# An SSM norm factor moved behind the projection, and the first weight chunk in pieces on two queues

## The chip, the cores and the metric

One core of one Trainium2 chip. The metric is the device time of one execution in microseconds; before and after are the medians of several runs.

## The reference, cut to what matters

The kernel computes a chain of float32 blocks over 256 tokens of width 1024. First comes an SSM layer with a pooling branch, then a SwiGLU feed-forward (ffn0), an attention layer, a second SwiGLU feed-forward (ffn1), a gated short convolution and a squared-ReLU MLP. The change is in the first layer:

```
proj = x @ w_in                                  # w_in: 1024 x 3088
u, z, xbc, dt = split(proj)
y_pool = multiscale_pool(u, pool_w, pool_scale)  # 256 x 512
y = ssd(xbc, dt, ...) + xh * d_skip              # 256 x 1024
y = y * silu(z)
y_ssm = y * rsqrt(mean(y*y, axis=-1) + 1e-6) * norm_w
h = concat([y_pool, y_ssm], axis=-1) @ w_out     # 1536 x 1024
x = layer_norm(ALPHA * x + h, g, b)              # ln0, then ffn0
```

The factor rsqrt(mean(y*y)) is one number per token, norm_w one number per channel.

## The kernel before

**Weights.** All weights pass through one list of chunks, mostly 1 MB each: either 1024 rows x 256 columns ("column chunk", 8 k tiles of 128 rows, in runs of 1 KB) or 256 rows x 1024 columns ("row chunk"). Chunk 0 is the dt part of w_in, 16 columns (64 KB, runs of 64 bytes); chunks 1 to 12 are the rest of w_in, 13 to 18 w_out (13, 14 the pool half, 15 to 18 the SSM half, called q = 0 to 3), 19 on ffn0. SyncE issues them in this order into four, later six slots, each when an earlier chunk's slot is free (L444 to L452). ScalarE copies each chunk rounded into `hi` (L1106), VectorE makes `lo = raw - hi` (L1519), both in program order by calls `split(n)`, "up to chunk n". TensorE makes three matmuls for each product: hi*hi, hi*lo, lo*hi (L551 to L563).

**Start.** SyncE issues x (two halves) and then chunks 0, 1, 2, 3. ScalarE issues the identity, two rows of vectors and the other constants (L1202 to L1205, 656 KB). GpSimd issues small vectors, two strided d_skip broadcasts (L482), the pooling weight (L484) and two lnrow broadcasts of 512 KB (L466). TensorE transposes x (L733), ScalarE and VectorE make x_hi and x_lo, and then come column blocks 0, 1, three small transposes and blocks 2 to 12 (`col`, L565). ScalarE evacuates each block, VectorE runs the convolution (L1740, L1742).

**End of the SSM stage.** PSUM banks 0 to 3 take the output of w_out, token-major: 128 tokens of half h in banks 2h and 2h+1. TensorE adds the pool rows first (`rows_full` of chunks 13 and 14, L851 and L857). VectorE finishes y (L1810) and multiplies by silu(z) (L1821). Then ScalarE squares (L1119), VectorE folds (L1535, L1538), TensorE sums over channels (L663), ScalarE takes the root (L1125), VectorE inverts (L1543), TensorE broadcasts the factor over partitions (L674), VectorE scales y (L1549), ScalarE makes x_hi with the gain (L1133), VectorE makes the full product and x_lo (L1567, L1558). Only then do the SSM rows run: half 0 over q = 0 to 3, then half 1, with the transposes of ln0's first half (`turn`, L647) ahead of the last twelve matmuls. ln0 itself is on VectorE (L1581 to L1601): `ALPHA * x + PSUM`, statistics, normalise. ffn0 opens with blocks of one token half at a time (`half_cols`, L581) in banks 6, 7 and 4, 5.

Of the kernel before, what the change touches and what calls it, by code (L numbers as in the profile page):

```python
# [11 lines left out]
P = 128  # L12
# [3 lines left out]
KT = D // P  # L16
# [53 lines left out]
def build(nc, A, out):  # L70
    ctx = ExitStack()
    with ctx:
# [25 lines left out]
        d_skip = sb("d_skip_sb", [P, KT])  # L98
        head_vec = sb("head_vec", [16, 4])
# [219 lines left out]
        def norm_incs(name, kind):  # L319

            pairs = NORM_TILES[name] // 2
            if kind == "folded":
# [13 lines left out]
        NORM_BANKS = {"qn": (7, 7), "kvn": (7, 7), "ssm": (5, 6)}  # L336
# [103 lines left out]
        def _(sp):  # L440
# [3 lines left out]
            for c in range(n_chunks):  # L444
# [16 lines left out]
        def _(pool):  # L461
# [14 lines left out]
            with nc.allow_non_contiguous_dma(reason="a few small vectors"):  # L476
# [72 lines left out]
        def _(pe):  # L549
# [15 lines left out]
            def col(c, bank, hi, lo, operand=None, between=None):  # L565
# [3 lines left out]
                pe.wait_ge(lo_split, c + 1)  # L569
                for m in range(0, n, P):  # L570
# [3 lines left out]
                    for k in range(kt):  # L574
                        if operand and m == 0 and k % 2 == 0:
# [36 lines left out]
            def rows_full(c, hi, lo, start):  # L612

                rows_part(c, hi, lo, 0, start)
                rows_part(c, hi, lo, 1, start)
# [69 lines left out]
            def ffn(name, operand, after, src):  # L685
# [8 lines left out]
                for h in range(2):  # L694
                    half_cols(g, 6 - 2 * h, h, operand)
                    half_cols(g + 1, 7 - 2 * h, h, operand, between=None if h else lambda: turn(operand, x_tok, 1, (0,)))
                    if h == 0:
                        turn(operand, x_tok, 1, (1,))
                for i in range(1, NF):
                    b = 4 + 2 * (i % 2)  # L700
# [8 lines left out]
                    if name == "ffn1" and i in MOD_AT:  # L709
                        pe.wait_ge(hid_done, o + i + 1)  # L710
                        mod_sums(MOD_AT[i], 4 + 2 * ((i - 1) % 2))
# [146 lines left out]
            norm_sums("ssm")  # L858
            norm_bcast("ssm")
            for h in range(2):  # L860
                for q in range(4):
# [3 lines left out]
                    if q < 3:  # L865
                        rows_half(base + 15 + q, x_hi[:, two, :], x_lo[:, two, :], h)
                    else:
                        if h:
                            turn("ln0", x_tok, 0)
# [1173 lines left out]
```

## Time and profile before

| | us |
|---|---|
| median of 3 runs | 1025.4 (1022.43 to 1026.02) |
| profiled execution | 1026.73 |
| its span | 1024.9 |
| TensorE matmul busy | 967.5 (94%) |
| TensorE weight load busy | 881.2 (86%) |
| VectorE busy | 645.9 (63%) |
| ScalarE busy | 462.3 (45%) |
| GpSimd busy | 60.5 (6%) |
| HBM read | 188.48 MB, 185 GB/s |

The mean granted TensorE clock is 0.973 of 2.4 GHz. Times within the profile are microseconds from the start of the span. A matmul's own duration overlaps the next one's; the distance between starts is what it costs in a row.

### The profile page before, as it was taken

The page shows a single profiled execution, that of the slowest core. Times are in us where ns is not written, and L with a number is a line of the kernel's source. Part 1 is how long each engine was busy: PE and PEld are TensorE (multiplying, and loading weights), DVE is VectorE, ACT ScalarE, POOL GpSimd, SP SyncE. Part 2 cuts the span into 40 slices and gives each one's busy share as a digit, 9 for nine tenths or more (in the row PEclk, how much of TensorE's full clock was granted, in tenths as well). Part 3 has the DMA queues.
Part 4 walks back from the last instruction along what each step waited for, and adds up shares of the span by engine and source line. Part 5 has one row for each costly group of instructions (what it writes and reads, how often), then busy time and mean ns, then how long its engine had stood idle before and what let it go on. Part 6 is the DMA issues. An engine that isn't in the chain of part 4 may idle for free.

```text
span 1024.9 us, 15132 instructions
## 1 busy us (share of the span) xinstructions
PE 967.5 (94%) x6565; PEld 881.2 (86%) x6565; DVE 645.9 (63%) x731; ACT 462.3 (45%) x550; POOL 60.5 (6%) x80
## 2 busy tenths in 40 slices
PE   3999969999999999999799999999899999999996
PEld 3999859999999899877589999898799888899884
DVE  2796687554545774456487877778867775445544
ACT  2655753443433454554454434435344544344432
POOL 3006000000000000020020100000000000000000
PEclk8999979999999999889999999999899999999999
DMA  9653336665655462321269999895565545655521
GB/s 204 210 165 124 124 123 214 201 202 172 198 174 196 125 206 78 113 83 44 81 211 341 374 335 341 305 349 209 165 205 170 159 141 193 201 179 191 184 104 42
DMA packets 122266, 190.51 MB, mean 186 GB/s; under 512 B 6566, under 2 KB 103064, under 8 KB 119128
## 3 DMA queue, kind: packets, MB, share of 16 engines
q1 hardware_dynamic: 116176, 157.00, 47.3%
q0 software_dynamic: 5648, 31.78, 9.1%
q8 instruction: 52, 0.85, 0.3%
q10 hardware_dynamic: 376, 0.77, 0.2%
q14 instruction: 14, 0.11, 0.0%
HBM read 188.48 MB, written 1.05 MB: 185 GB/s over the span
## 4 chain that ended last, share of the span: by engine, by line
PE 80%; DVE 10%; ACT 5%; DMA 2%; issue 2%; SPq 0%; DVEq 0%; POOL 0%; ACTq 0%
PE PS L554 15%; PE PS L556 15%; PE PS L555 15%; PE PS L561 10%; PE PS L562 9%; PE PS L563 9%; DVE lo L1519 4%; ACT hi L1106 2%; DMA raw<-even_w_in 2%; PE PS L647 1%; PE PS L682 1%; PE PS L998 1%; PE PS L974 1%; ACT hid L1386 1%; DMA sq<-norm_gains 1%
## 5 line engine op out<-in xcount | busy, mean ns | idle before, releaser
L1519 DVE TENSOR_TENSOR lo<-raw,hi 128x2048 fp32r<-128x2048 f32 (+2 forms) x151 | 338.3, 2259 | 166.9 <-ACT hi L1106 166.5
L554 PE MATMUL PS<-x_hi,hi 128*128 128x256 f32 x1320 | 376.3, 285 | 10.6 <-DVE lo L1519 10.6
L555 PE MATMUL PS<-x_lo,hi 128*128 128x256 f32 x1320 | 373.9, 283 | 0.0
L556 PE MATMUL PS<-x_hi,lo 128*128 128x256 f32 x1320 | 373.8, 283 | 0.0
L1106 ACT ACTIVATE hi<-raw 128x2048 fp32r<-128x2048 f32 (+2 forms) x151 | 279.5, 1880 | 14.8 <-DMA raw<-even_w_in 14.8
L554 PEld LDWEIGHTS PS<-x_hi,hi 128*128 128x128 f32 x1320 | 253.3, 192 | 13.0 <-DVE lo L1519 11.0
L555 PEld LDWEIGHTS PS<-x_lo,hi 128*128 128x128 f32 x1320 | 253.3, 192 | 1.9 <-issue 0.5
L556 PEld LDWEIGHTS PS<-x_hi,lo 128*128 128x128 f32 x1320 | 253.2, 192 | 0.0
L561 PE MATMUL PS<-hi,hid_hi 128*128 128x512 f32 x352 | 141.4, 402 | 6.1 <-DVE lo L1519 5.6
L563 PE MATMUL PS<-hi,hid_lo 128*128 128x512 f32 x352 | 138.8, 394 | 0.0
L562 PE MATMUL PS<-lo,hid_hi 128*128 128x512 f32 x352 | 138.8, 394 | 0.0
L561 PE MATMUL PS<-hi,x_hi 128*128 128x256 f32 (+1 forms) x256 | 83.6, 327 | 9.2 <-DVE x_lo L1558 5.0
L561 PEld LDWEIGHTS PS<-hi,hid_hi 128*128 128x128 f32 x352 | 66.3, 188 | 23.3 <-issue 9.6
L562 PE MATMUL PS<-lo,x_hi 128*128 128x256 f32 (+1 forms) x256 | 81.4, 318 | 0.0
L563 PE MATMUL PS<-hi,x_lo 128*128 128x256 f32 (+1 forms) x256 | 81.4, 318 | 0.0
L563 PEld LDWEIGHTS PS<-hi,hid_lo 128*128 128x128 f32 x352 | 66.2, 188 | 15.4
L562 PEld LDWEIGHTS PS<-lo,hid_hi 128*128 128x128 f32 x352 | 66.2, 188 | 14.9 <-issue 1.2
L561 PEld LDWEIGHTS PS<-hi,x_hi 128*128 128x128 f32 x256 | 50.5, 197 | 15.5 <-issue 6.3
L1191 ACT ACTIVATE gate_s<-PS 128x512 f32<-128x512 f32 x20 | 12.0, 598 | 103.6 <-PE PS L556 103.6
L563 PEld LDWEIGHTS PS<-hi,x_lo 128*128 128x128 f32 x256 | 50.2, 196 | 2.9
L562 PEld LDWEIGHTS PS<-lo,x_hi 128*128 128x128 f32 x256 | 50.3, 197 | 2.7
L1196 ACT ACTIVATE hid_hi<-hid 128x512 fp32r<-128x512 f32 x20 | 12.6, 632 | 80.6 <-DVE hid L1686 80.6
(273 smaller groups left out, 842.5 us busy)
## 6 DMA issues: line engine op xcount, KB each, us to landing
raw<-ffn_w_gate SPq DMA_DIRECT2D x22, 1024.0 KB, 5.6
raw<-ffn_w_up SPq DMA_DIRECT2D x22, 1024.0 KB, 5.5
raw<-ffn_w_down SPq DMA_DIRECT2D x22, 1024.0 KB, 5.4
raw<-mlp_w_in SPq DMA_DIRECT2D x16, 1024.0 KB, 5.7
raw<-mlp_w_out SPq DMA_DIRECT2D x16, 1024.0 KB, 4.9
raw<-even_w_in SPq DMA_DIRECT2D x12, 1024.0 KB, 5.5
sq<-ada_w POOLq DMA_DIRECT2D x12, 1024.0 KB, 6.5
r<-ada_w POOLq DMA_DIRECT2D x12, 1024.0 KB, 7.4
```

The source lines that it names most:

```text
L554: pe.matmul(dst, wh, hi, start=start, stop=False, skip_group_check=True)
L555: pe.matmul(dst, wh, lo, start=False, stop=False, skip_group_check=True)
L556: return pe.matmul(dst, wl, hi, start=False, stop=stop_, skip_group_check=True)
L561: pe.matmul(dst, hi, wh, start=start, stop=False, skip_group_check=True)
L562: pe.matmul(dst, hi, wl, start=False, stop=False, skip_group_check=True)
L563: return pe.matmul(dst, lo, wh, start=False, stop=stop_, skip_group_check=True)
L647: last = pe.transpose(PS[:, 2 * h + n, j * P:(j + 1) * P], src[:, h, o:o + P], ident)
L682: last = pe.matmul(PS[:, bank + n, :], ones[:, :], modrow[:, m, n * HB:(n + 1) * HB], start=True, stop=True)
L1106: act.activation(split_view("hi", c), split_view("raw", c), ACT.Copy).then_inc(hi_split, 1)
L1191: act.activation(gate_s[:, i % 2, :, :], bank2(4 + 2 * (i % 2)), ACT.Silu).then_inc(silu, 1)
L1196: act.activation(hid_hi[:, i % 3, :, :], hid[:, i % 2, :, :], ACT.Copy).then_inc(hi_done, 1)
L1519: dve.tensor_tensor(split_view("lo", c), split_view("raw", c), split_view("hi", c).bitcast(F32), ALU.subtract)\
```

## The change

Two parts, and what they need:

1. **Norm factor.** x_hi and x_lo are made from y times the gain, without the factor. The SSM rows go to banks 4 to 7, apart from the pool rows in 0 to 3. VectorE adds the pool rows to ALPHA * x (`pool_added`), and ln0's sum becomes `PSUM * rstd + x_tok`, with the factor per token. The sum over channels is done beside the projection; the broadcast, the scaling and the `full` product are gone. q = 0 runs as a whole for both halves before the others. ScalarE makes its splits of chunks 17 to 20 before the root. ffn0 and ffn1 use banks 4/5 and 6/7 in exchanged order.
2. **Start.** Chunk 0 is issued on ScalarE's queue after the identity, and split ahead of x_hi and x_lo. Chunk 1 is loaded in four pieces of two k tiles on SyncE's queue, each with its own semaphore; the splits and block 1 follow piece by piece. The other constants are issued after split 1; the pooling weight (and with it lnrow) after the first evacuation. d_skip is loaded as one row of 16 to all partitions and sorted by two copies on VectorE.

```diff
 sync:
-            for c in range(n_chunks):
+            for c in range(1, n_chunks):
+                if c == 1:
+                    for i in range(4):
+                        ks = slice(2 * i, 2 * i + 2)
+                        sp.dma_start(slot("raw", 1)[:, ks, :], chunks[1][0][:, ks, :])\
+                          .then_inc(raw_landed[slot_of[1]] if i == 3 else sem(f"piece_landed{i}"), 16)
+                    continue
 gpsimd:
-                for e in range(2):
-                    pool.dma_start(d_skip[64 * e:64 * e + 64, :],
-                                   A["d_skip"][0:1, e::2].to_broadcast([64, KT])).then_inc(sem("heads_landed"), 16)
-            pool.dma_start(pool_w_sb[:, :, :], A["pool_w"][0].rearrange("g c d -> c g d")).then_inc(sem("poolw_landed"), 16)
+                pool.dma_start(d_heads[:, :], A["d_skip"][0:1, :].to_broadcast([P, HEADS])).then_inc(sem("d_landed"), 16)
...
+            pool.wait_ge(sem("even_evac"), 1)
+            pool.dma_start(pool_w_sb[:, :, :], A["pool_w"][0].rearrange("g c d -> c g d")).then_inc(sem("poolw_landed"), 16)
             ln_rows("ln0")
 tensor:
-            norm_sums("ssm")
-            norm_bcast("ssm")
+            pe.wait_ge(*norm("ssm", "lo", 1))
+            rows_full(base + 15, x_hi[:, 0:2, :], x_lo[:, 0:2, :], True, b0=4)
             for h in range(2):
-                for q in range(4):
+                for q in range(1, 4):
...
                     if q < 3:
-                        rows_half(base + 15 + q, x_hi[:, two, :], x_lo[:, two, :], h)
+                        rows_half(base + 15 + q, x_hi[:, two, :], x_lo[:, two, :], h, b0=4)
+                        continue
+                    if h:
+                        turn("ln0", x_tok, 0)
                     else:
...
+                        pe.wait_ge(sem("pool_added"), 1)
+                        norm_sums("ssm")
+                    rows_end(base + 15 + q, x_hi[:, two, :], x_lo[:, two, :], h, "even_out", b0=4)
 scalar:
             act.dma_start(const[:, 0:P], A["consts"][:, 0:P]).then_inc(sem("ident_landed"), 16)
+            act.dma_start(slot("raw", 0), chunks[0][0]).then_inc(raw_landed[slot_of[0]], 16)
...
-            act.dma_start(const[:, P:], A["consts"][:, P:]).then_inc(sem("const_landed"), 16)
+            split(0)
             for b in range(4):
...
+            split(1)
+            act.dma_start(const[:, P:], A["consts"][:, P:]).then_inc(sem("const_landed"), 16)
             split(2)
...
             split(first["even_out"] + 2)
-            squares(r, KT, (sem("gated"), 0))
+            for q in range(4):
+                act.wait_ge(sem("gated"), q + 1)
+                for k in (2 * q, 2 * q + 1):
+                    act.activation(x_hi[:, k, :], r[:, k, :], ACT.Identity, scale=vec(1, 4 + k)).then_inc(sem("norm_hi"), 1)
+            split(first["even_out"] + 3)
+            squares(r)
+            split(first["ffn0"] + 1)
             norm_std("ssm")
-            split(first["even_out"] + 3)
-            operand_hi("ssm", r, x_hi, lambda k: vec(1, 4 + k))
 vector, ln_sum:
+                    acc = PS[:, b0 + 2 * h + n, :]
+                    if which == "even_out":
+                        dve.wait_ge(*norm("ssm", "rcp", 1))
+                        dve.wait_ge(sem("pool_added"), 4)
+                        dve.scalar_tensor_tensor(out=half(r_tok, h, n), in0=acc, scalar=rstd[:, 2 + h:3 + h],
+                                                 in1=half(x_tok, h, n), op0=ALU.mult, op1=ALU.add).then_inc(sig(name, "r"), 1)
+                        continue
 vector, even_y:
+                if j == 0:
+                    dve.wait_ge(sem("d_landed"), 16)
+                    for e in range(2):
+                        ins = dve.tensor_copy(d_skip[64 * e:64 * e + 64, :], d_heads[64 * e:64 * e + 64, e::2])
+                    link(ins)
+                if j:
+                    split(first["even_out"] + 2)
 vector, after the gating:
-            split(first["even_out"] + 2)
+            def ssm_low(q):
...
+                for k in (2 * q, 2 * q + 1):
+                    ins = dve.scalar_tensor_tensor(out=x_lo[:, k, :], in0=r[:, k, :], scalar=vec(1, 4 + k),
+                                                   in1=x_hi[:, k, :].bitcast(F32), op0=ALU.mult, op1=ALU.subtract)
+                ins.then_inc(sem("norm_lo"), 1)
+            ssm_low(0)
+            ssm_low(1)
+            split(first["even_out"] + 3)
+            ssm_low(2)
+            ssm_low(3)
+            dve.wait_ge(chunk_used, first["even_out"] + 2)
+            for h in range(2):
+                for n in range(2):
+                    dve.scalar_tensor_tensor(out=half(x_tok, h, n), in0=half(x_tok, h, n), scalar=ALPHA, in1=PS[:, 2 * h + n, :],
+                                             op0=ALU.mult, op1=ALU.add).then_inc(sem("pool_added"), 1)
+            split(first["even_out"] + 4)
             fold_squares("ssm")
+            split(first["ffn0"] + 1)
             inverse_std("ssm")
-            split(first["even_out"] + 3)
-            dve.wait_ge(*norm("ssm", "rb", 1))
-            operand_tail("ssm", r, sq, x_hi, x_lo, lambda k: vec(1, 4 + k))
-            layer_norm("ln0", "even_out", "ffn0")
+            layer_norm("ln0", "even_out", "ffn0", b0=4)
```

## Rows read from the trace of the kernel before

**Rows 1.** The page, part 4: the chain that ended last, by engine.
```profile
PE 80%; DVE 10%; ACT 5%; DMA 2%; issue 2%; SPq 0%; DVEq 0%; POOL 0%; ACTq 0%
```

**Rows 2.** The chain in order of time: start, duration, what.
```profile
2.12 18.83 DMA raw<-even_w_in
20.96 1.92 ACT hi L1106
```

**Rows 3.** Windows, opening: stretch, its length, busy by engine, PEclk, DMA share, GB/s.
```profile
2.00:11.00 9.00, 3.49 (x16) 3.27 (x16) 2.30 (x4) 4.00 (x6) 7.70 (x17) 1.00 1.36 319
11.00:19.00 8.00, 4.63 (x24) 4.43 (x24) 1.69 (x2) 0.62 (x1) 0.00 (x0) 0.79 0.59 10
25.30:30.00 4.70, 4.70 (x22) 4.70 (x23) 0.74 (x1) 2.00 (x2) 0.00 (x0) 0.50 1.09 351
34.00:100.00 66.00, 66.00 (x561) 64.58 (x561) 54.70 (x85) 38.42 (x52) 17.16 (x16) 1.00 0.51 160
```

**Rows 4.** d_skip: its two issues (timeline), and the time from issue to landing.
```profile
6.14 1.45 POOL L482 DMA_DIRECT2D d_skip_sb<-d_skip  x2
...
DMA to landing us min/median/max: 8.7/11.5/14.2
```

**Rows 5.** Timeline of the opening: start, us, engine, line, operation, [idle before].
```profile
6.55 3.49 PE L733 MATMUL PS<-const,x_tok 128*128 128x128 f32 x16 [6.55 <-DMA x_tok<-x]
7.67 0.60 ACT L1209 ACTIVATE x_hi<-PS 128x512 fp32r<-128x512 f32 x1 [3.67 <-PE PS L733]
...
33.79 0.38 PE L554 MATMUL PS<-x_hi,hi 128*128 128x256 f32 x1
```

**Rows 6.** Timeline of the boundary.
```profile
125.62 2.50 DVE L1821 TENSOR_TENSOR r<-r,z_silu 128x512 f32<-128x512 f32 x4
...
140.85 0.79 PE L561 MATMUL PS<-hi,x_hi 128*128 128x512 f32 x1 [5.03 <-DVE x_lo L1558]
...
155.96 1.28 DVE L1581 SCALAR_TENSOR_TENSOR r<-x_tok,PS 128x512 f32<-128x512 f32 x2
...
160.24 1.42 DVE L1601 SCALAR_TENSOR_TENSOR x_tok<-r,rstd,lnrow 128x512 f32<-128x512 f32 x2
...
166.92 0.28 PE L561 MATMUL PS<-hi,x_hi 128*128 128x256 f32 x1
```

**Rows 7.** DMA: chunk 0 (size, us to landing); SyncE's chunk issues before 60 us.
```profile
raw<-even_w_in SPq DMA_DIRECT2D x1, 64.0 KB, 7.2
...
DMA to landing us min/median/max: 5.3/7.0/24.5
```

**Rows 8.** Windows at full rate, with holes, and after the holes.
```profile
149.50:163.30 13.80, 13.72 (x60) 11.32 (x61) 12.05 (x13) 3.41 (x4) 0.00 (x0) 1.00 0.31 94
497.20:501.80 4.60, 2.39 (x12) 1.39 (x11) 3.01 (x15) 2.03 (x8) 0.00 (x0) 0.94 0.01 4
501.80:504.60 2.80, 2.80 (x8) 2.15 (x8) 0.72 (x3) 0.96 (x5) 0.00 (x0) 0.50 0.00 0
```

**Rows 9.** Timeline of VectorE, two waits for TensorE late in the SSM stage.
```profile
102.99 1.29 DVE L1769 TENSOR_TENSOR hid<-PS,tok 128x512 f32<-128x512 f32 x2 [3.20 <-PE PS L793]
...
122.72 1.12 DVE L1810 SCALAR_TENSOR_TENSOR r<-xbc,d_skip_sb,PS 128x128 f32<-128x128 f32 x4 [2.50 <-PE PS L832]
```

**Rows 10.** Groups by line, several stretches: operation, count, busy us, mean ns.
```profile
L1742 DVE SCALAR_TENSOR_TENSOR conv_acc<-conv_in,vecs,conv_acc 128x256 f32<-128x256 f32 x36 | 15.9, 482 | 0.6
...
L1519 DVE TENSOR_TENSOR lo<-raw,hi 128x2048 fp32r<-128x2048 f32 x6 | 13.5, 2287 | 2.6 <-ACT hi L1106 2.6
...
L1106 ACT ACTIVATE hi<-raw 128x2048 fp32r<-128x2048 f32 x7 | 13.0, 1906 | 0.0
L1133 ACT ACTIVATE x_hi<-r,vecs 128x256 fp32r<-128x256 f32 x8 | 3.6, 500 | 5.5 <-DVE r L1549 5.5
```

**Rows 11.** SyncE from 90 to 190 us: chunk 20's issue; landings of all issues there.
```profile
131.25 0.53 SPq L452 DMA_DIRECT2D raw<-ffn_w_up  x1
...
DMA to landing us min/median/max: 4.8/5.5/10.0
```

More of the change, by code:

```diff
@@ L321, in norm_incs @@
             pairs = NORM_TILES[name] // 2
+            if name == "ssm" and kind in ("rb", "scaled", "full"):
+                return 0
             if kind == "folded":
@@ L568, in col @@
                 n *= copies
-                pe.wait_ge(lo_split, c + 1)
+                if c != 1:
+                    pe.wait_ge(lo_split, c + 1)
                 for m in range(0, n, P):
@@ L574, in col @@
                     for k in range(kt):
+                        if c == 1 and m == 0 and k == 6:
+                            pe.wait_ge(lo_split, 2)
+                        elif c == 1 and m == 0 and k % 2 == 0:
+                            pe.wait_ge(sem("lo_piece"), k // 2 + 1)
                         if operand and m == 0 and k % 2 == 0:
@@ L694, in ffn @@
                 for h in range(2):
-                    half_cols(g, 6 - 2 * h, h, operand)
-                    half_cols(g + 1, 7 - 2 * h, h, operand, between=None if h else lambda: turn(operand, x_tok, 1, (0,)))
+                    half_cols(g, 4 + 2 * h, h, operand)
+                    half_cols(g + 1, 5 + 2 * h, h, operand, between=None if h else lambda: turn(operand, x_tok, 1, (0,)))
                     if h == 0:
@@ L865, in _ @@
                     if q < 3:
-                        rows_half(base + 15 + q, x_hi[:, two, :], x_lo[:, two, :], h)
-                    else:
-                        if h:
-                            turn("ln0", x_tok, 0)
-                        rows_end(base + 15 + q, x_hi[:, two, :], x_lo[:, two, :], h, "even_out")
+                        rows_half(base + 15 + q, x_hi[:, two, :], x_lo[:, two, :], h, b0=4)
+                        continue
+                    if h:
+                        turn("ln0", x_tok, 0)
+                    else:
+                        pe.wait_ge(sem("pool_added"), 1)
+                        norm_sums("ssm")
+                    rows_end(base + 15 + q, x_hi[:, two, :], x_lo[:, two, :], h, "even_out", b0=4)
             ffn("ffn0", "ln0", "ln1", x_tok)
@@ L1104, in split @@
                     c = done[0]
+                    if c == 1:
+                        for i in range(4):
+                            ks = slice(2 * i, 2 * i + 2)
+                            act.wait_ge(raw_landed[slot_of[1]] if i == 3 else sem(f"piece_landed{i}"), 16)
+                            act.activation(slot("hi", 1)[:, ks, :], slot("raw", 1)[:, ks, :], ACT.Copy)\
+                               .then_inc(hi_split if i == 3 else sem("hi_piece"), 1)
+                        done[0] += 1
+                        continue
                     act.wait_ge(raw_landed[slot_of[c]], landed_at[c])
@@ L1517, in split @@
                     c = done[0]
+                    if c == 1:
+                        for i in range(4):
+                            ks = slice(2 * i, 2 * i + 2)
+                            dve.wait_ge(*((hi_split, 2) if i == 3 else (sem("hi_piece"), i + 1)))
+                            dve.tensor_tensor(slot("lo", 1)[:, ks, :], slot("raw", 1)[:, ks, :],
+                                              slot("hi", 1)[:, ks, :].bitcast(F32), ALU.subtract)\
+                               .then_inc(lo_split if i == 3 else sem("lo_piece"), 1)
+                        done[0] += 1
+                        continue
                     dve.wait_ge(hi_split, c + 1)
@@ L1542, in inverse_std @@
                 dve.wait_ge(*norm(name, "std", 1))
-                dve.reciprocal(rstd[:, 0:2], std[:, :]).then_inc(sem("norm_rcp"), 1)
+                o = 2 if name == "ssm" else 0
+                dve.reciprocal(rstd[:, o:o + 2], std[:, :]).then_inc(sem("norm_rcp"), 1)
             def scale_pair(name, q, src, dst):
@@ L1703, in _ @@
             dve.memset(conv_in[:, :, :, 0:3], 0.0).then_inc(sem("conv_pad"), 1)
+            split(0)
             for b in range(4):
```

32 lines of the change are left out of this document (18 added, 14 removed).

## The prediction

> **What bounds the kernel.** I read the chain that ended last first. TensorE holds four fifths of it, almost all in matmuls that run back to back [rows 1]. A saving must come from where TensorE stands or runs at half rate, and the change touches two such places: the opening, and the end of the SSM stage.
>
> **The opening.** The chain begins with one transfer, the first full weight chunk (chunk 1, 1 MB), which lands at 20.96; its split follows, 1.92 us on ScalarE [rows 2] and 2.29 on VectorE [rows 10], and TensorE starts on it at 25.25. The windows say that this is no matter of bandwidth: from 2 to 11 us the queues moved 319 GB/s (2.9 MB: x, the constants, chunk 0, most of chunk 1), then 10 GB/s from 11 to 19, then 351 and the like again [rows 3]. The hole fits the two d_skip transfers, 2 KB each in 512 runs of 4 bytes, issued at 6.1 and 6.9: they land 8.7 and 14.2 us after issue, at 14.8 and 21.1 [rows 4]. So chunk 1 was nearly through at 11 and waited for small change. Its matmuls then run at half rate, 22 in 4.7 us (0.214 each), where the stretch from 34 to 100 us has 561 in 66 us (0.118) and no idle time [rows 3]. Block 2 starts at 33.79 [rows 5].
>
> **The end of the SSM stage.** The gating multiplies end at 128.1; the projection of the SSM part starts at 140.85 and the feed-forward at 166.92 [rows 6]. Between the pool rows, which end at 130.1, and the feed-forward lie 96 matmuls, 0.23 us each at full rate (60 in 13.8 us [rows 8]): 22 us of work in 36.8 us. The rest is the chain of squares, fold, sums, root, reciprocal, broadcast and scaling ahead of every operand, and its half-rate aftermath.
>
> **Part 1, the start.** Gone from ahead of chunks 1 to 3: 656 KB of constants (issued after split 1 now), the d_skip pair (now one transfer of 128 runs of 64 bytes), pool_w and the two lnrow loads (after the first evacuation now). Before chunk 1 is complete remain x, the identity, chunk 0 and chunk 1, 2.2 MB: from 2.3 us at 319 GB/s they end near 9.2, seen near 10. So the operand sets the pace. The transposes run from 6.55 for 3.5 us, x_hi starts at 7.67 [rows 5]. Chunk 0 is now split on ScalarE ahead of x_hi. It took 7.2 us from issue, behind 1 MB of x [rows 7]; now issued near 1.2 on its own queue it lands between 6.5, with x (no delay), and 8.4 (with 1.05 us of split, x_hi is 1.8 us late). I take the first, since it no longer stands behind x, and 0.4 us for what it takes from x.
> The Trainium skill, "DMA: Bandwidth & Descriptors", section "Issuing engines are not separate DMA queues", speaks against a gain from two queues: all run on the same 16 engines and interleave. That page's measured table gives 64 KB 0.95 us; by it, as an estimate, x would be 0.95 us later and the saving 0.5 us smaller.
> Transposes end at 10.4. Block 0 (24 matmuls) follows them; I let TensorE stay at half rate until 12.0 (8 at 0.214), then 16 at 0.118: 14.0. The pieces of chunk 1 are split on ScalarE by 13.5 and on VectorE by 14.2, each pair of k tiles ahead of its use. Whole, chunk 1 would be ready near 15.5, so the pieces are worth some 1.5 us of this. Block 1: 48 at 0.118, 19.7; the three small transposes 0.5. Block 2 starts at 20.3 instead of 33.79: **13.5 us**. Chunks 2 and 3 make it 4.3 MB in all, landed by 15.9 at 319 to 351 GB/s, split on VectorE by 17.8 and 20.9: in time for 20.3 and 26. Bounds: block 2 at 19.2 (x not delayed, full rate from the transposes on), 14.6 saved; at 22.2 (x_hi 1.8 late), 11.6 saved. From here to 100 us TensorE has no idle time [rows 3], so everything keeps its distance.
> At no cost: the two tiny copies of d_skip on VectorE, which a little later waits 3.20 us for TensorE; split 15, moved ahead of the second y loop, 2.2 us where VectorE waited 2.50 [rows 9]. It ends at 123.5, so the gating ends 0.2 later. Were the covers gone, 0.5 and 2.2 us. The pooling weight and lnrow are needed after 100 us, and the queues carry 160 GB/s until then [rows 3].
>
> **Part 2, the boundary, in the old time base.** TensorE no longer waits for the norm. After the pool rows (130.1) come the rows of q=0 (24 matmuls, to 135.7) and q=1 (12, to 138.5). What is late next is VectorE, added up from 128.3: eight gain-and-subtract over 256 columns, 0.45 each as the taps of the convolution step (3.6); five chunk splits, 2.2 each by step (11.1) [rows 10]; four pool additions, 0.6 each as the two in 1.28 us (2.5); the fold, four operations of the gating's kind, 0.62 each (2.5) [rows 6]; 1.9 waiting for ScalarE's half of split 16, since ScalarE makes eight x_hi first (0.46 by step, 126.4 to 130.1) and then 1.9 [rows 10]; 0.7 for the reciprocal and gaps. Sum 22.3: 150.6. Then ln0 of the first half, which ran from 155.96 to 161.66, 5.7 us [rows 6]: 156.3. A turn and the 12 last matmuls follow: 159.7.
> TensorE gets holes on the way: 2.2 us for split 17 (ready 140.7), 1.0 for split 18 (145.5), 1.7 for ln0. Between 497.2 and 501.8 it was busy 2.39 of 4.6 us, and was then granted 0.50, 1.2 GHz, for 2.8 us [rows 8]. I take such a stretch here: the first half's last 12 matmuls end 2.4 us later, at 150.7, which VectorE (150.6) hardly feels; TensorE then reaches the turn at 156.3 and ends at **160.0**. 166.9 - 160.0 = **6.9 us**.
> The Trainium skill, "TensorE: Matmul & The Clock Gate", Part 1, has the clock follow how busy the array lately was, so that a hole costs twice; this rule speaks against a boundary made of small holes. By that rule, the trace agrees.
> Bounds: 8.0 if the clock holds and VectorE has no gaps; 3.5 if a half-rate stretch falls on the second half too (2.4) and split 20 is 1 us late. TensorE alone would end at 153.4; VectorE's sum excludes it. ScalarE's root now stands behind its splits of chunks 17 to 20. Chunk 20 is issued at 131.25, and landings there take 4.8 to 10.0 us [rows 11]: 141.3, split by 143.2, root with its table load 145, some 5 us before VectorE asks. The exchanged banks (4/5 for 6/7) have the same counts and waits: nothing.
>
> **Sum.** The profiled execution took 1026.73 us for a span of 1024.9. 1026.73 - 13.5 - 6.9 = 1006.3. The median of the runs, 1025.4, is 1.3 lower: **1005.0 us**. By its own bounds this case runs from 1002 to 1010.
>
> **Rivals.** (A) The hole stays: 128 reads of one 64-byte row hold the queues as d_skip did. For: the transfer keeps its place in GpSimd's queue, and no row shows what made d_skip slow. Against: an eighth of the runs. Chunk 1 is through before 11, but chunk 2 then has 0.6 MB moved, resumes at 19.2, lands near 21 and is split at 25: block 2 starts at 25.2, 8.6 saved, 1010 in all. (B) The boundary pays little: VectorE is the bound there, and each of its waits now delays TensorE one for one. At 3 saved, 1009. (C) More than I see: 14.6 and 8.0 saved, 1002 or just below. (D) The other side: chunk 0 on ScalarE's queue. Its 1024 runs of 64 bytes do what the 4-byte ones did, and as its split stands ahead of x_hi, the whole kernel waits for it one for one. It decides if chunk 0 lands 20.4 us after x, near 27, and at 32 gives 1030. Against: it took 7.2 us before; for: landings of up to 24.5 us are there at the start, with the hole in them [rows 7]. (E) The constants, issued near 13.6, are awaited by TensorE before block 2: they are there at 20.6 if they take 7 us, but at 10 us, the longest of the boundary [rows 11], TensorE waits 3.3 us: 1008.
>
> **Chances.** Forecast 0.60, A 0.14, B 0.12, C 0.05, E 0.04, D 0.05 (0.03 beyond +0.5%, 0.02 about no change). Some 0.5%, 5 us, is what a measurement here can tell from no change. The range, 1001 to 1011, takes in the forecast's bounds, A, B and E.
>
> **What would show it.** No hole in the DMA rate between 11 and 19 us (else A). Chunk 0 split on ScalarE before 7.7 (else D). Chunk 1's matmuls from near 14, block 2 near 20.3. At the boundary VectorE busy with one wait of 1.9 us, TensorE waiting on splits 17 and 18 and on ln0, none of over 1 us on the sums, and 30 us instead of 36.8 from the end of the pool rows to the feed-forward. I am wrong if block 2 starts after 23 or if that distance is over 33.

## The result, and the profile after

The kernel after takes **1008.42 us** (median of 6 runs, 1005.3 to 1010.03); the kernel before took 1026.11 beside it (1022.43 to 1027.55). The ratio is 0.9825, 95% interval 0.9808 to 0.9843: 1.75% faster. The profiled execution took 1008.01 us for a span of 1006.2, with a mean granted TensorE clock of 0.988 (0.973 before). Against the profiled execution of before, 1026.73, that is 18.7 us; the working had said 20.4.

The page, part 4, the chain that ended last by engine, answers to [rows 1]. The DMA share has halved, since the chain no longer starts with 19 us of transfer:

```profile
PE 79%; DVE 11%; ACT 6%; issue 2%; DMA 1%; DVEq 0%; ACTq 0%; POOL 0%
```

**The opening.** Windows of the kernel after, the stretches of [rows 3] (columns: stretch, length, busy by engine, PEclk, DMA share, GB/s):

```profile
2.00:11.00 9.00, 3.65 (x16) 3.27 (x16) 1.01 (x1) 3.38 (x5) 5.05 (x13) 1.00 1.05 310
11.00:19.00 8.00, 7.04 (x46) 7.07 (x47) 7.60 (x11) 6.11 (x9) 0.00 (x0) 1.00 0.93 308
...
25.30:30.00 4.70, 4.70 (x42) 4.70 (x41) 4.63 (x8) 1.92 (x4) 1.05 (x2) 1.00 1.06 334
```

The hole from 11 to 19 us is gone: 308 GB/s instead of 10. TensorE runs 46 matmuls there instead of 24, and at 25.3 to 30 it is at full rate, 42 in 4.7 us instead of 22.

What sets the pace now is chunk 0. DMA issues of the first 20 us (size, us from issue to landing), then the timeline of the opening, which answers to [rows 5] and [rows 7]:

```profile
raw<-even_w_in ACTq DMA_DIRECT2D x1, 64.0 KB, 7.7
d_heads<-d_skip POOLq DMA_DIRECT2D x1, 8.0 KB, 5.3
```
```profile
1.18 0.45 ACTq L1227 DMA_DIRECT2D raw<-even_w_in  x1
...
6.25 3.65 PE L746 MATMUL PS<-const,x_tok 128*128 128x128 f32 x16 [6.25 <-DMA x_tok<-x]
...
8.90 1.06 ACT L1130 ACTIVATE hi<-raw 128x1024 fp32r<-128x1024 f32 x1 [4.47 <-DMA raw<-even_w_in]
9.87 0.58 ACT L1234 ACTIVATE x_hi<-PS 128x512 fp32r<-128x512 f32 x1
...
11.96 0.55 PE L562 MATMUL PS<-x_hi,hi 128*128 128x256 f32 x1 [2.07 <-DVE x_lo L1756]
...
```

Chunk 0, 64 KB, is issued at 1.18 on ScalarE's queue and seen at 8.90, after 7.7 us. Its split stands ahead of x_hi, which therefore starts at 9.87 instead of 7.67. TensorE has finished its transposes at 9.9 and stands for 2.07 us. Here are the first matmuls of block 0, the last slow ones and the start of block 2:

```profile
12.74 0.41 PE L562 MATMUL PS<-x_hi,hi 128*128 128x256 f32 x1
12.95 0.41 PE L563 MATMUL PS<-x_lo,hi 128*128 128x256 f32 x1
...
15.30 0.32 PE L562 MATMUL PS<-x_hi,hi 128*128 128x256 f32 x1
15.46 0.28 PE L563 MATMUL PS<-x_lo,hi 128*128 128x256 f32 x1
...
22.26 0.47 PE L755 MATMUL PS<-const,vec_rows 60*128 60x60 f32 x3
22.67 0.39 PE L562 MATMUL PS<-x_hi,hi 128*128 128x256 f32 x1
```

The starts are 0.21 us apart until 15.30, 0.12 from there on: half rate and full rate. (The PEclk column of the window 11:19 reads 1.00 all the same. The first clock record in this trace stands at 15.4 us, and a stretch ahead of it reads 1.00 for want of one; here only the distance between starts tells.) Block 2 starts at 22.67 instead of 33.79 [rows 5]: **the start gave 11.1 us**.

**The boundary.** Timeline of VectorE and TensorE, the kernel after; it answers to [rows 6] (all times are 11 us earlier than before by the start alone). Behind it stands a window of the same kernel, from 134.9 to 138.4 us:

```profile
114.60 2.50 DVE L1877 TENSOR_TENSOR r<-r,z_silu 128x512 f32<-128x512 f32 x4
117.02 1.67 DVE L1885 SCALAR_TENSOR_TENSOR x_lo<-r,vecs,x_hi 128x256 fp32r<-128x256 f32 x4
120.48 2.29 DVE L1559 TENSOR_TENSOR lo<-raw,hi 128x2048 fp32r<-128x2048 f32 x1 [1.79 <-ACT hi L1130]
122.69 1.67 DVE L1885 SCALAR_TENSOR_TENSOR x_lo<-r,vecs,x_hi 128x256 fp32r<-128x256 f32 x4
124.27 2.48 DVE L1897 SCALAR_TENSOR_TENSOR x_tok<-x_tok,PS 128x512 f32<-128x512 f32 x4
126.66 2.29 DVE L1559 TENSOR_TENSOR lo<-raw,hi 128x2048 fp32r<-128x2048 f32 x1
...
131.52 6.69 DVE L1559 TENSOR_TENSOR lo<-raw,hi 128x2048 fp32r<-128x2048 f32 x3
...
138.38 1.41 DVE L1626 SCALAR_TENSOR_TENSOR r<-PS,rstd,x_tok 128x512 f32<-128x512 f32 x2
...
142.79 1.41 DVE L1649 SCALAR_TENSOR_TENSOR x_tok<-r,rstd,lnrow 128x512 f32<-128x512 f32 x2
```
```profile
129.09 0.47 PE L569 MATMUL PS<-hi,x_hi 128*128 128x512 f32 x1 [1.82 <-DVE lo L1559]
...
133.86 0.50 PE L569 MATMUL PS<-hi,x_hi 128*128 128x512 f32 x1 [1.42 <-DVE lo L1559]
...
143.79 1.13 PE L660 MATMUL PS<-const,x_tok 128*128 128x128 f32 x8
...
147.52 0.28 PE L569 MATMUL PS<-hi,x_hi 128*128 128x256 f32 x1
```
```profile
134.90:138.40 3.50, 3.50 (x10) 2.72 (x9) 3.40 (x4) 0.00 (x0) 0.00 (x0) 0.52 0.00 0
```

VectorE goes through the queue that the prediction had listed, with the one wait for ScalarE (1.79 us) and hardly a gap. TensorE waits for splits 17 and 18 (1.82 and 1.42), then runs at half rate for 3.5 us (granted clock 0.52), and reaches the turn at 143.79 without a wait. From the start of the gating multiplies to the feed-forward's first matmul it is 147.52 - 114.60 = 32.9 us, where it was 166.92 - 125.62 = 41.3 [rows 6]: **the boundary gave 8.4 us**. Together, less 0.1 lost between block 2 and the gating, 19.4 us; the span is 18.7 shorter, so 0.7 is given back later. Counted between table loads of ScalarE, marks that both kernels have, the lead falls by 0.5 us between 150 and 327 us of the kernel after, grows by 1.35 up to 693 and falls by 1.5 behind it. Of the edits only the exchanged banks of the feed-forwards reach in there.

### The profile page after: what moved, and what is told of

The parts are those of the page before. It is cut to its first block, busy times and chain, and to the rows that moved or that the text cites. A ratio compares the mean times of both kernels' runs of the same rounds, so it can differ in the third digit from the quotient of the medians.

```text
span 1006.2 us, 15135 instructions
## 1 busy us (share of the span) xinstructions
PE 962.0 (96%) x6561; PEld 876.1 (87%) x6561; DVE 644.7 (64%) x732; ACT 461.5 (46%) x553; POOL 59.4 (6%) x79
## 4 chain that ended last, share of the span: by engine, by line
PE 79%; DVE 11%; ACT 6%; issue 2%; DMA 1%; DVEq 0%; ACTq 0%; POOL 0%
PE PS L562 15%; PE PS L564 15%; PE PS L563 15%; PE PS L569 9%; PE PS L570 9%; PE PS L571 9%; DVE lo L1559 4%; ACT hi L1130 2%; PE PS L695 1%; PE PS L660 1%; DMA raw<-even_w_in 1%; ACT hid L1417 1%; DVE r L1629 1%; PE PS L1014 1%; DMA sq<-norm_gains 1%
## 5 line engine op out<-in xcount | busy, mean ns | idle before, releaser
L570 PE MATMUL PS<-lo,hid_hi 128*128 128x512 f32 x352 | 139.8, 397 | 0.0
L569 PEld LDWEIGHTS PS<-hi,hid_hi 128*128 128x128 f32 x352 | 66.6, 189 | 23.9 <-issue 9.5
L571 PEld LDWEIGHTS PS<-hi,hid_lo 128*128 128x128 f32 x352 | 66.5, 189 | 15.4
```

The lines of the kernel that those rows point to most:

```text
L569: pe.matmul(dst, hi, wh, start=start, stop=False, skip_group_check=True)
L570: pe.matmul(dst, hi, wl, start=False, stop=False, skip_group_check=True)
L571: return pe.matmul(dst, lo, wh, start=False, stop=stop_, skip_group_check=True)
```

## The experiments

All are compared with runs of the kernel before on the same chip (medians 1026.02 for e1 to e4, 1025.51 for e5, e6, e7 and e9, 1024.14 for e8, e10, e11 and e12). Two marks are read from each profile: the start of block 2, and the distance from the start of gating to ffn0. The second repeats within 0.02 us in the seven kernels with the boundary of the kernel after (32.9), and within 0.03 in the three with the old one (41.3). The first doesn't repeat as well: the kernel after, e1, e8 and e9 have the same opening, and their block 2 starts at 22.67, 22.64, 24.07 and 22.40. A difference in block 2 of less than 1.7 us therefore needs a look at the rows behind it. (In e6 and e10 the split of chunk 0 stands behind two x_hi, so that its start isn't the landing.)

| kernel | chunk 0 split at | block 2 at | gating to ffn0 | span | median |
|---|---|---|---|---|---|
| before | 10.57 | 33.79 | 41.3 | 1024.9 | 1026.11 |
| after | 8.90 | 22.67 | 32.9 | 1006.2 | 1008.42 |
| e1 start alone | 8.52 | 22.64 | 41.3 | 1016.9 | 1016.31 |
| e2 boundary alone | 10.66 | 33.18 | 32.9 | 1012.8 | 1014.72 |
| e3 d_skip alone | 10.57 | 23.70 | 41.3 | 1015.5 | 1019.26 |
| e4 after, old d_skip | 8.49 | 25.84 | 32.9 | 1010.3 | 1012.13 |
| e5 chunk 1 whole | 8.82 | 23.54 | 32.9 | 1009.7 | 1009.92 |
| e6 split 0 in mid | 8.81 | 22.27 | 32.9 | 1004.0 | 1005.66 |
| e7 filler | 8.17 | 20.43 | 32.9 | 1002.1 | 1004.42 |
| e8 split 17 first | 9.43 | 24.07 | 33.8 | 1006.7 | 1008.52 |
| e9 splits late | 8.32 | 22.40 | 30.8 | 1004.3 | 1006.13 |
| e10 e6 + filler + e9 | 8.69 | 20.50 | 30.8 | 1003.8 | 1004.09 |
| e11 e7 + e9 | 8.55 | 20.81 | 30.8 | 1005.3 | 1006.57 |
| e12 chunk 0 on SyncE | 8.46 | 22.43 | 32.9 | 1004.2 | 1006.02 |

### The two parts apart (e1, e2)

e1 is the kernel before with the hunks of the start, e2 with those of the boundary:

```diff
 e1, of the change only:
+ chunk 0 on ScalarE's queue, split(0) ahead of x_hi, chunk 1 in pieces,
+ constants after split(1), one d_skip transfer, pool_w after the first evacuation
 e2, of the change only:
+ x_hi/x_lo without the factor, pool_added, banks 4 to 7, q = 0 for both halves,
+ ln0's sum with rstd, the new order of splits, banks exchanged in ffn0 and ffn1
```

> The kernel before with part 1 of the change alone (the start); the end of the SSM stage is the old one. Theory: the two parts add. Block 2 starts at 22.7 us as in the changed kernel (33.79 before), so 11.1 us less: 1015 us. Rival: the earlier start is given back at the old boundary, because the chunks 15 to 18 or the pooling weight come no earlier: then 1018 or more.

> The changed kernel with the old start (chunk 1 whole on SyncE behind chunk 0, constants early, d_skip as two strided transfers, pooling weight and lnrow early). Theory: the boundary saves 8.3 us on its own: 1018 us. Rival: the boundary's saving needs the new start, and less than 6 us is seen: 1020 or more.

e1: 1016.31 us (1014.8 to 1018.71), ratio 0.9915, 0.9886 to 0.9944. e2: 1014.72 (1014.53 to 1018.18), ratio 0.9908, 0.9879 to 0.9937. The parts add up where they were made: e1 moves block 2 by 11.15 us and leaves the boundary at 41.3, e2 moves the boundary to 32.9 and block 2 by 0.6. In the times they add up as well within their scatter: 9.7 and 11.3 saved, 21.0 together, against 17.7 in both at once. e2 came out 3 us better than expected, e1 1 us worse, and together they promise 3 us more than the kernel after has. That difference lies far behind both edits. The stretch from 346 to 713 us of the kernel before, from one table load of ScalarE to another, took 367.2 us in before, 368.4 in e1, 363.8 in e2, 365.8 in the kernel after. From 404 to 440 us the two differ in the granted clock (windows of e1, then e2):

```profile
404.00:440.00 36.00, 32.85 (x196) 28.11 (x194) 17.47 (x47) 20.17 (x42) 4.51 (x3) 0.81 0.27 88
```
```profile
404.00:440.00 36.00, 32.53 (x231) 28.73 (x230) 19.22 (x53) 23.30 (x48) 4.51 (x3) 0.95 0.26 93
```

e1 changes nothing there and e2 only the banks of ffn1, and the banks don't explain it: e3, with the old ones, took 364.4 us, e5 and e8, with the new ones, 366.9 and 362.3. Which stretches run at 1.2 GHz comes out differently from kernel to kernel. Whether the new position in time or chance decides it was not tried; by these numbers it puts several us of scatter on every sum made from local gains. Which of the edits of the boundary carries its 8.4 us, the factor behind the projection or the new order of splits, was not taken apart either; e2 shows them together.

### What made the hole (e3, e4)

```diff
 e3, on the kernel before:
-                for e in range(2):
-                    pool.dma_start(d_skip[64 * e:64 * e + 64, :],
-                                   A["d_skip"][0:1, e::2].to_broadcast([64, KT])) ...
+                pool.dma_start(d_heads[:, :], A["d_skip"][0:1, :].to_broadcast([P, HEADS])) ...
 e4, on the kernel after: the same edit backwards
```

> The kernel before with one edit: d_skip comes as one transfer of 128 runs of 64 bytes, sorted by two copies. Theory (the 4-byte runs make the hole from 11 to 19 us): the DMA rate stays above 250 GB/s from 11 to 19 us, chunk 1 lands near 11.5, block 1 follows block 0 at 17.3 and block 2 starts near 25, 8.8 us less: 1017 us. Rival 1 (the hole comes from the queue order, the constants or the lnrow loads): hole and time stay, 1026. Rival 2 (the broadcast of one row is as slow): the same 1026.

> The changed kernel with the old pair of strided d_skip transfers put back in the same place of GpSimd's queue. Theory: the hole is back between 11 and 19 us. Chunk 1 is through by then, chunk 2 is not: its split waits until about 21, block 2 starts near 25 instead of 22.7: 1011 us. Rival: in the new order of queues the pair does no harm, 1008.

e3: 1019.26 us (1015.97 to 1027.1), ratio 0.9942, 0.9917 to 0.9967. e4: 1012.13 (1011.51 to 1015.93), ratio 0.988, 0.9849 to 0.9911. Windows of e3, then of e4:

```profile
11.00:19.00 8.00, 6.07 (x37) 6.07 (x38) 4.04 (x3) 2.88 (x3) 0.00 (x0) 0.79 1.06 365
```
```profile
11.00:19.00 8.00, 7.45 (x50) 7.48 (x51) 4.60 (x8) 2.57 (x6) 0.00 (x0) 0.79 0.57 16
```

One edit switches the hole on and off: 365 GB/s with a single transfer of 64-byte runs, everything else as before; 16 GB/s with the two strided ones, everything else as after. 4 KB in 4-byte runs all but stop the queues for 8 us. (The edit changes several things at once, above all the stride, the length of the runs and their number, 1024 against 128; which of them does it was not taken apart.) In e3 block 2 starts at 23.70, 10.1 us earlier: of the 11.1 us of the start, this one edit brings 10.1. The last one is there at block 0 already, which starts at 12.93 in e3 and at 11.96 in the kernel after, each time right behind its operands: in e3 chunk 0 is split behind x_hi, at 10.57, in the kernel after ahead of it, at 8.90. In time e3 shows less than its 10.1: its median is 6.8 us below that of before, over ten runs from 1015.97 to 1027.1, its profiled execution 9.5 us below. In e4 chunk 1 is through before the hole, chunk 2 is caught in it, and TensorE waits 3.54 us for its split ahead of block 2. What rival A feared of the new transfer, e4 shows of the old one; the new form is harmless (landed after 5.3 us).
The Trainium skill, "DMA: Bandwidth & Descriptors", section "Rules for kernel authors", says that a strided last dimension becomes one descriptor for each element. The trace agrees in so far as the strided form is the slow one: it landed 8.7 and 14.2 us after issue [rows 4], the contiguous one after 5.3.

### The rest of the start (e5, e6, e7, e12)

```diff
 e5, on after: chunk 1 in one transfer and one split, block 1 behind it
 e6, on after (ScalarE and VectorE alike):
-            split(0)
             for b in range(4):
+                if b == 2:
+                    split(0)
 e7, on after, TensorE, behind the transposes of x:
+            for i in range(9):
+                pe.transpose(PS[:, 6, (i % 4) * P:(i % 4) * P + P], ident, ident)
 e12, on after:
-            act.dma_start(slot("raw", 0), chunks[0][0]) ...
+            sp.dma_start(slot("raw", 0), chunks[0][0]) ...      (behind x, ahead of chunk 1)
```

> The changed kernel with chunk 1 loaded and split whole; all else of the new start stays. Theory (the operand of block 0 sets the pace, the pieces matter little): chunk 1 has landed by 10.5, ScalarE splits it from 11.8 to 13.7, VectorE by 16.0; block 0 ends at 16.0 to 16.5, so block 2 starts at 22.7 to 22.9, at most 0.3 us later than in the changed kernel: 1008.5 us. Rival (my term in the prediction): the pieces are worth some 1.5 us, block 2 starts at 24.2, 1010 us.

> The changed kernel with the split of chunk 0 between the second and the third pair of x tiles on ScalarE and VectorE, instead of ahead of all. Theory (x_hi waits for chunk 0, which lands 7.7 us after its issue): x_hi starts near 7.5 instead of 9.87, block 0 near 11.2 instead of 11.96, block 2 near 21.9 instead of 22.67: 1007.5 us. Rival: chunk 0's landing bounds block 0 in any order, and block 2 stays at 22.7.

> The changed kernel with nine transposes of the identity on TensorE between the transposes of x and block 0; nobody reads them. They fill the 2.07 us in which TensorE waits for its operand. Theory (the half-rate stretch of block 0, 11.96 to 15.4, follows that wait): block 0 runs at full rate, some 15 matmuls gain 0.09 us each, block 2 starts at 21.3 instead of 22.67: 1007 us. Rival (TensorE is granted half rate at its first longer work whatever comes ahead): block 0 is as slow, block 2 at 22.7.

> The kernel after with chunk 0 issued on SyncE's queue again, right behind x, instead of on ScalarE's. If the 64-byte runs set its landing (7.2 us on SyncE's queue, 7.7 on ScalarE's), it lands some 7.2 us after an issue about 0.2 to 0.7 us later, so near 9.0, block 0 within 0.6 us of 11.96, and the time stays within 1 us of 1008.4: the second queue buys nothing. Rival, the second queue matters: landing over 1.5 us later, the time over 1010.

**e5**: 1009.92 us (1006.34 to 1011.5), ratio 0.9855, 0.9822 to 0.9887. Block 2 at 23.54, 0.9 later than in the kernel after, between what the two theories said. But the rows give this to the clock and not to the pieces. Timeline of e5 (VectorE's splits of chunks 1 and 2, the first matmul of block 1, the first at full rate), then the last slow matmul of e8, which has the pieces:

```profile
13.65 4.49 DVE L1537 TENSOR_TENSOR lo<-raw,hi 128x2048 fp32r<-128x2048 f32 x2
...
17.14 0.41 PE L562 MATMUL PS<-x_hi,hi 128*128 128x256 f32 x1
...
17.53 0.28 PE L564 MATMUL PS<-x_hi,lo 128*128 128x256 f32 x1
```
```profile
17.75 0.35 PE L562 MATMUL PS<-x_hi,hi 128*128 128x256 f32 x1
```

Chunk 1, in one piece, is split by 15.95, and block 1 follows block 0 at 17.14 without a wait. What is longer is the half-rate stretch: 25 matmuls 0.21 apart instead of 15, 10 times 0.1 us. e8 has 25 as well, with the pieces, and block 2 at 24.07. So in this opening the pieces bring nothing that shows. They would where block 0 ends earlier than that, as in e7, whose block 1 starts at 14.18; that was not tried.

**e6**: 1005.66 (1003.1 to 1008.43), ratio 0.9818, 0.978 to 0.9856. Block 0 starts at 11.17, 0.8 earlier, but at half rate as before (19 matmuls), and block 2 only 0.4 earlier; the theory had 21.9, the rival 22.7. e9, with the order of the kernel after and a chunk 0 seen at 8.32, has block 2 at 22.40, so 0.1 to 0.4 is all that can be put down to the edit. The half rate ends at 15.5 to 15.9 in e1, e6, e9, e12 and the kernel after, while block 0 starts anywhere from 11.17 to 11.96: what starts earlier runs longer at half rate, and half of the gain is lost.

**e7**: 1004.42 (1003.95 to 1009.41), ratio 0.9817, 0.9782 to 0.9851. The nine extra matmuls compute nothing that is used. Timeline of TensorE in e7, then in e12, whose chunk 0 came at nearly the same time as e11's (below):

```profile
9.60 1.34 PE L749 MATMUL PS<-const 128*128 128x128 f32 x9
11.23 0.36 PE L562 MATMUL PS<-x_hi,hi 128*128 128x256 f32 x1 [0.29 <-DVE x_lo L1758]
11.66 0.28 PE L562 MATMUL PS<-x_hi,hi 128*128 128x256 f32 x1
12.02 0.28 PE L562 MATMUL PS<-x_hi,hi 128*128 128x256 f32 x1
```
```profile
11.52 0.55 PE L563 MATMUL PS<-x_hi,hi 128*128 128x256 f32 x1 [1.40 <-DVE x_lo L1756]
11.87 0.42 PE L564 MATMUL PS<-x_lo,hi 128*128 128x256 f32 x1
```

With TensorE kept at work from 9.6 to 11.0, block 0 runs at full rate from its second matmul (starts 0.36 apart for three), and block 2 starts at 20.43, 2.2 us before the kernel after. 0.7 of this is a chunk 0 that happened to land earlier in this profile; e11 has the same filler with chunk 0 seen at 8.55, and block 2 at 20.81, where e12 with chunk 0 at 8.46 and no filler has 22.43: the clock alone is worth 1.6 us here, some 17 slow matmuls in e12 at 0.1 us each. Over the kernels without filler there are 15 to 25 of them, and the pause alone doesn't set them: in e4 the first seven behind a pause of 1.98 us start 0.12 to 0.19 apart, and 0.21 only from 12.46 on.
The Trainium skill, "TensorE: Matmul & The Clock Gate", Part 1, has the default state throttled and lets sustained activity release it. The trace agrees: 3.65 us of transposes, 2.07 us of nothing and then half rate in the kernel after, a pause of 0.29 us and full rate in e7.

**e12**: 1006.02 (1005.57 to 1008.77), ratio 0.9826, 0.9804 to 0.9849. Chunk 0, issued 0.46 us later and behind x, was seen at 8.46, earlier than the 8.90 on its own queue. DMA issues of e12, size and us to landing:

```profile
raw<-even_w_in SPq DMA_DIRECT2D x1, 64.0 KB, 6.8
```

The second queue buys nothing. Over the kernels that issue chunk 0 on ScalarE's queue it takes 7.0 to 8.2 us from issue to landing, and on SyncE's 6.8 to 7.8 (before, e2, e3, e12): about the same for either. The size isn't what takes the time: the 656 KB of constants landed 6.3 us after issue in the kernel after.

### The boundary (e8, e9)

```diff
 e8, on after, VectorE:
+            split(first["even_out"] + 4)
             dve.wait_ge(chunk_used, first["even_out"] + 2)
             ... the four pool additions
-            split(first["even_out"] + 4)
 e9, on after: split 17 as in e8; 18 ahead of the fold, 19 behind it,
 20 behind ln0's first half (was: 18, 19 and 20 all between fold and reciprocal);
 on TensorE the sums over channels behind the first half's last rows, not ahead of them
```

> The kernel after, with VectorE's split of chunk 17 ahead of the four pool additions instead of behind them; nothing else moved. TensorE's wait of 1.82 us at 129.09 should vanish. If VectorE's queue sets the end of the boundary, the same work stays in it, the next wait of TensorE (1.42 us, on chunk 18) grows by what the first one lost, and from the end of the gating to ffn0 it stays 30.4 us, the time within 1 us of the kernel after (1008.4). If TensorE's holes set it, 1.8 us go, 1006.6.

> The changed kernel with another order at the boundary: VectorE splits chunk 17 ahead of the pool additions and chunk 18 ahead of the fold, chunk 19 after it, and chunk 20 only behind ln0's first half; TensorE makes the sums behind the first half's last rows. Theory (VectorE's queue sets the end of the boundary): ln0's first half begins 2.2 us earlier counted from the end of the gating, and the feed-forward begins 28.1 us after the gating instead of 30.4: 1006 us. Rival 1 (TensorE's holes before splits 17 and 18, 1.8 and 1.4 us, set it): 3.2 us less. Rival 2 (ScalarE's root is then late, or the second half of ln0 waits): no gain, 1008.5.

**e8**: 1008.52 us (1007.53 to 1011.45), ratio 0.9852, 0.9821 to 0.9883. The first wait is gone, and 1.85 us turn up at the sums instead. Timeline of TensorE in e8 and the window behind it:

```profile
133.25 0.58 PE L676 MATMUL PS<-ones,hid 128*128 128x1 f32 x4 [1.85 <-DVE hid L1578]
...
135.36 0.79 PE L569 MATMUL PS<-hi,x_hi 128*128 128x512 f32 x1 [1.54 <-DVE lo L1559]
...
146.19 1.03 PE L660 MATMUL PS<-const,x_tok 128*128 128x128 f32 x8
```
```profile
133.00:138.00 5.00, 3.22 (x10) 2.67 (x11) 5.00 (x4) 2.27 (x5) 0.00 (x0) 0.59 0.19 59
138.00:141.00 3.00, 3.00 (x9) 2.29 (x8) 2.65 (x4) 0.00 (x0) 0.00 (x0) 0.54 0.00 0
```

VectorE's queue is as long as it was (from gating to ln0's sum 23.9 us, 23.8 in after), but the two holes now lie close together, the stretch at half rate is longer, and TensorE, not VectorE, is late at the turn: 33.8 us instead of 32.9. Neither theory had that. The first one's bound of 1 us holds for the time, but by luck: block 2 came 1.4 us later with an unchanged opening, the boundary took 0.9 more, and the later stages gave 1.8 of this back (at ffn0's first matmul e8 is 2.3 us behind the kernel after, at the end 0.5).

**e9**: 1006.13 (1004.36 to 1010.61), ratio 0.9829, 0.9794 to 0.9864. One of VectorE's five splits, that of chunk 20, leaves the queue ahead of ln0's first half. Timeline of VectorE and TensorE in e9:

```profile
114.34 2.50 DVE L1879 TENSOR_TENSOR r<-r,z_silu 128x512 f32<-128x512 f32 x4
...
136.03 1.41 DVE L1626 SCALAR_TENSOR_TENSOR r<-PS,rstd,x_tok 128x512 f32<-128x512 f32 x2
```
```profile
131.14 0.47 PE L569 MATMUL PS<-hi,x_hi 128*128 128x512 f32 x1 [1.43 <-DVE lo L1559]
...
141.23 1.32 PE L660 MATMUL PS<-const,x_tok 128*128 128x128 f32 x8 [1.20 <-DVE x_tok L1649]
...
145.16 0.28 PE L569 MATMUL PS<-hi,x_hi 128*128 128x256 f32 x1
```

From gating to ln0's sum 21.7 us instead of 23.8. TensorE has one hole of 1.43 us and no stretch at half rate (the granted clock is 1.00 from 130 to 139.8), and now waits 1.20 for ln0. Feed-forward after 30.8 us instead of 32.9: 2.1 us, of which TensorE loses 0.4 at once, since it waits 0.41 for ln0's second half.

In the kernel after both engines reached the turn together, 143.8: VectorE by its queue, TensorE by two holes and the half-rate stretch. Which of them is the limit, e2, e5 and e6 show, where the clock stayed up over the same boundary with the same two holes (1.8 and 1.4 us). e6, the window up to the turn and TensorE's turn:

```profile
130.00:143.20 13.20, 10.51 (x48) 8.34 (x46) 12.90 (x16) 3.69 (x6) 0.00 (x0) 1.00 0.38 120
```
```profile
143.20 1.32 PE L660 MATMUL PS<-const,x_tok 128*128 128x128 f32 x8 [1.27 <-DVE x_tok L1650]
```

Without the half-rate stretch TensorE only waits 1.27 us for ln0, and the feed-forward still starts 32.9 us after the gating (e2 and e5: 1.28 and the same 32.9). So VectorE's queue is the limit; what TensorE gets back there gives nothing, and the 2.1 of e9 come from the split that left the queue.

### The combinations (e10, e11)

```diff
 e10: e6, six filler transposes, e9
 e11: e7 (nine filler transposes), e9
```

> The kernel after with all three edits that helped alone: chunk 0 split between the pairs of x_hi, six filler transposes on TensorE ahead of block 0, VectorE's boundary splits later and the sums behind the first half's rows. By their traces alone: block 2 at 20.2 (2.5 us earlier), the boundary 2.2 us shorter, together 4.7 us off 1008.4: 1003.7. If the start's edits overlap and the gain is lost again behind the boundary, not below 1005.

> The kernel after with nine filler transposes and the later boundary splits, chunk 0's split where it was. Theory: 2.2 us at the start and 2.2 at the boundary add, 1004.0. Rival: the boundary's gain was another clock episode and not the order of VectorE's work; then 1006.

e10: 1004.09 us (1002.58 to 1006.12), ratio 0.9806, 0.9783 to 0.9829. e11: 1006.57 (1002.91 to 1008.65), ratio 0.9821, 0.9795 to 0.9847. Block 2 at 20.50 and 20.81, boundary 30.8 in both: the local gains are there in full, and at ffn0's first matmul e10 is 4.3 and e11 4.0 us ahead of the kernel after. 0.5 goes at once, most of it in the wait for ln0's second half, and nothing more up to 400 us. In e11 one us goes between 400 and 494 us, and both lose 1.4 to 1.5 behind 693 us, where the granted clock of the last windows is 0.97 instead of 1.00 (the kernel after, then e10):

```profile
940.00:1002.00 62.00, 57.02 (x317) 48.89 (x315) 28.84 (x25) 22.26 (x23) 0.00 (x0) 1.00 0.29 94
```
```profile
940.00:1002.00 62.00, 54.62 (x298) 46.77 (x297) 28.10 (x25) 21.66 (x22) 0.00 (x0) 0.97 0.25 88
```

e11's time is what its rival named (1006), but not for the rival's reason, a boundary that gains nothing. e10 has the largest local gains, but its interval and that of the kernel after overlap, so it isn't shown to beat it; that it beats the kernel before is.

## Why the prediction was right, point by point

The forecast was 1005.0 us with a range of 1001 to 1011, and faster; it measured 1008.42. The likeliest case happened in its main mechanisms, the hole that goes and the norm that leaves TensorE's path, and two terms of its sum were mis-sized in opposite directions: 13.5 for the start measured 11.1, and 6.9 for the boundary measured 8.3 to 8.4. That 2.4 too much and 1.4 too little partly cancel is luck.

**The hole.** "The hole fits the two d_skip transfers": right, and the whole of it (e3, e4). Rivals A, D and E didn't happen: no hole, chunk 0 at 8.90 and not 27, the constants landed 6.3 us after issue, and nothing waits for them. Nor did B, with 8.4 saved at the boundary, and of C only the boundary's half. (C's own sum, 14.6 and 8.0 saved, gives 1002.8, not "1002 or just below".)

**Chunk 0's landing was the term that failed.** The step took 6.5, "with x (no delay)", "since it no longer stands behind x". It came at 8.90, later than even the late bound of 8.4, and not because of what stood ahead of it (e12 has it behind x, at 8.46). The sign that the prediction had set, a split before 7.7 or else rival D, was missed without D: the landing came 2.4 us later than the 6.5 assumed, not 20. So x_hi was 2.2 us late, and the first matmul of block 0 came at 11.96 instead of 10.4: 1.6 us.

**The half-rate stretch** was to end at 12.0, after 8 matmuls. It ended at 15.3, after 15: 0.8 us. TensorE had stood for 2.07 us just before, and e7 and e11, which fill that pause, have no such stretch. Block 0 ends at 16.4 instead of 14.0, and these 2.4 us are the whole miss of the start: behind it everything ran as worked out, block 1 in 5.7 us and the three small transposes in 0.6. Block 2 at 22.67 lies 0.5 outside the bound of 22.2, which had the late x_hi but not the low clock behind it; e7, which takes that away, starts block 2 at 20.43, where the forecast had it. That a pause is followed by half rate was in the prediction at the boundary, and was not applied to the opening. The sign "wrong if block 2 starts after 23" was kept by 0.3 us, and not safely: e8, with the same opening, has 24.07.

**The pieces** were put at 1.5, for a block 0 that ends at 14.0. It ended at 16.4, with even the whole chunk 1 split by 15.95 (e5), so they bring nothing that shows; the constants, the pooling weight, split 15 and d_skip's copies cost nothing that shows: the distance from block 2 to the gating is 91.9 us in the kernel after and 91.8 before.

**The boundary.** The order and the single wait came as listed. VectorE's sum, 22.3, measured 138.38 - 117.1 = 21.3, by distances between starts: gain-and-subtract 3.2 for 3.6, splits 11.0 for 11.1, the pool additions 2.4 for 2.5, the fold 2.7 for 2.5, the wait 1.8 for 1.9, and 0.3 for the reciprocal and gaps where 0.7 was put. ln0 up to the turn took 5.4 for 5.7, and the gating did not end the 0.2 later that split 15 was to cost. This puts the turn 1.5 us earlier, which is what the boundary gave beyond 6.9 (1.4, counted from block 2); 8.3 lies just above the bound of 8.0. TensorE's holes, 2.2 and 1.0, measured 1.82 and 1.42; the third, 1.7 for ln0, is not there in the kernel after and is 1.3 in e2, e4, e5 and e6; the half-rate stretch was foreseen at its place and cost TensorE 1.6 instead of 2.4 (8 matmuls at 0.43). That it came at all is in part luck: the same two holes bring it in the kernel after, e7 and e12 and not in e2, e5 and e6. From turn to feed-forward 3.7 for 3.7. That VectorE hardly feels it holds, and only just: TensorE reached the turn in the same moment; in e8, with a longer half-rate stretch, it came 1 us later than that, and in e6, without one, the feed-forward starts no earlier. 28.6 us from the end of the pool rows (118.9) to the feed-forward, against the 30 given.

**The sum.** 1026.73 - 11.1 - 8.3 = 1007.3, and the profiled execution took 1008.01; 0.7 was given back behind both edits (0.5 lost up to 327 us, 1.35 gained up to 693, 1.5 lost behind), and why these stretches differ isn't settled. So 1005.0 was low by 3.4 us. Half of it, 1.7, is the sum for one profiled execution (1006.3 against 1008.01: 2.4 from the start and 0.7 from the later stages, less 1.4 from the boundary). The other half is the step from there to the median, 1.3 down in the forecast, 0.4 up in the runs.

## What to carry to other kernels

Look first for a stretch in which all queues stand still, and in it for a transfer in 4-byte runs: one such edit brought 10 of the 19 us that the two parts gained where they were made. A small transfer that the first operand waits for is priced by its latency (6.8 to 8.2 us here), not by its size or its queue, so nothing that others need should stand behind it in an engine's program. When TensorE has to wait a little ahead of a long run, work thrown away in that pause can be worth more than an earlier operand (1.6 us against 0.4 at most). Where two engines reach a point together, find out which one is the limit before relieving it: here TensorE's half-rate stretch was worth nothing, a split less in VectorE's queue 2.1 us. And before a difference between two profiles is put down to an edit, compare it with kernels that share the edited stretch: the same opening gave block 2 at 22.40 and at 24.07.

## What the runs showed of the hardware that was not expected

- Two transfers of 2 KB in 4-byte runs brought the rate of all queues from 310 or more to 10 to 16 GB/s for 8 us (before, e2, e4); the same values in 64-byte runs did nothing of the kind (after, e3).
- 64 KB in 64-byte runs landed 6.8 to 8.2 us after issue in all fourteen kernels, on either queue, beside x or behind it; 656 KB took 6.3 (after).
- Nine useless transposes in a pause of TensorE's took the half-rate stretch behind it away and 1.6 us with it, though all they do is fill time.
- The half-rate stretch of the same opening was 15 to 25 matmuls long (after, e1, e8, e9), which moved block 2 by up to 1.7 us together with a chunk 0 seen from 8.32 to 9.43. It is not in the clock column, since the trace of the kernel after has no clock record ahead of 15.4 us; the distance between starts, 0.21 us, tells.
- A stretch of 367 us in the later stages differed by up to 6 us between kernels (362.3 in e8, 368.4 in e1) with its parts at 1.2 GHz.
